# A hybrid layer with 32 experts on one core: the rows of the first four experts picked by one-hot products instead of gathered

## What is computed

```python
h = h + (merged @ w_out) * valid[None, :, None]
xn2 = rms_norm(h, norm2_w).reshape(B * T, D)
y_ffn = hier_moe(xn2, router_group, router_expert, expert_w_gate, expert_w_up, expert_w_down)
return h + y_ffn.reshape(B, T, D) * valid[None, :, None]

def hier_moe(xn, router_group, router_expert, w_gate, w_up, w_down):
    g_logits = xf @ router_group
    g_idx = jnp.argmax(g_logits, axis=-1)
    e_logits = ...                          # the 8 experts of the chosen group
    top_v, top_i = lax.top_k(e_logits, 2)
    for g in range(4):
        hg = silu(einsum('nd,edf->nef', xn, w_gate[g])) * einsum('nd,edf->nef', xn, w_up[g])
        y = y + einsum('nef,efd->nd', hg * combine[:, g, :, None], w_down[g])
```

## Time and profile before

| | |
|---|---|
| median of 3 runs | 680.68 us (679.83 to 681.95) |
| profiled execution | 684.17 us, its span 682.4 us |
| mean granted TensorE clock | 0.979 |
| busy share: PE, PEld, DVE, ACT, POOL | 95%, 73%, 56%, 30%, 15% |
| HBM read and written | 139.67 MB, 4.19 MB |
| chain that ended last, by engine | PE 86%, DVE 7%, ACT 3%, DMA 2%, issue 2% |

### The profile page before, as it was taken

One profiled execution on the slowest core, in us unless ns is written; L12 is line 12 of the kernel. 1 busy time (PEld: TensorE's weight loads), 2 busy tenths in 40 slices (PEclk: granted clock), 3 DMA queues, 4 the chain that ended last, 5 costly groups with the idle time before them and its releaser, 6 DMA issues.

```text
span 682.4 us, 11048 instructions
## 1 busy us (share of the span) xinstructions
PE 650.3 (95%) x4419; PEld 499.7 (73%) x4419; DVE 383.4 (56%) x729; ACT 202.2 (30%) x426; POOL 104.4 (15%) x142
## 2 busy tenths in 40 slices
PE   4999999999999999999999976999999999999997
PEld 2579999998888888888789963665757575656564
DVE  3648334678897878776764463452525344351514
ACT  5337132224534344432433350212020202010111
POOL 3300006899300000000000011110101001010010
PEclk9699999999999999999999995999999999999999
DMA  7431212301231111211553028999999999999953
GB/s 238 144 123 52 74 62 76 112 1 62 85 101 62 62 63 62 62 62 62 175 205 145 33 70 341 396 414 405 409 407 407 411 396 422 402 418 388 420 214 123
DMA packets 50086, 139.32 MB, mean 204 GB/s; under 512 B 6355, under 2 KB 28388, under 8 KB 41845
## 3 DMA queue, kind: packets, MB, share of 16 engines
q1 hardware_dynamic: 47298, 134.37, 51.6%
q0 software_dynamic: 2592, 4.20, 1.7%
q10 hardware_dynamic: 146, 0.07, 0.1%
HBM read 139.67 MB, written 4.19 MB: 211 GB/s over the span
## 4 chain that ended last, share of the span: by engine, by line
PE 86%; DVE 7%; ACT 3%; DMA 2%; issue 2%; POOL 0%; ACTq 0%; DVEq 0%; POOLq 0%
PE bank L917 17%; PE bank L583 12%; PE bank L584 12%; PE bank L585 12%; PE bank L930 8%; PE bank L1035 8%; PE bank L799 1%; DVE y_lo L1770 1%; PE bank L591 1%; PE bank L826 1%; PE bank L823 1%; PE bank L592 1%; ACT whi L1142 1%; DMA xg<-rows_hbm,row_no 1%; DVE sig_a L1504 1%
## 5 line engine op out<-in xcount | busy, mean ns | idle before, releaser
L1435 DVE TENSOR_TENSOR wlo<-wraw,whi 128x2048 fp32r<-128x2048 f32 (+1 forms) x25 | 56.5, 2258 | 19.8 <-ACT whi L1142 19.8
L583 PE MATMUL bank<-xhi,whi 128*128 128x512 f32 x160 | 64.5, 403 | 0.0
L583 PE MATMUL bank<-whi,xhi 128*128 128x256 f32 x224 | 64.4, 288 | 0.0
L584 PE MATMUL bank<-xlo,whi 128*128 128x512 f32 x160 | 63.3, 396 | 0.0
L584 PE MATMUL bank<-wlo,xhi 128*128 128x256 f32 x224 | 63.0, 281 | 0.0
L585 PE MATMUL bank<-whi,xlo 128*128 128x256 f32 x224 | 62.9, 281 | 0.0
L585 PE MATMUL bank<-xhi,wlo 128*128 128x512 f32 x160 | 62.9, 393 | 0.0
L917 PE MATMUL bank<-wgate,xgT 128*64 128x256 f32 x512 | 61.0, 393 | 1.3 <-DVE xgT L1728 1.0
L917 PE MATMUL bank<-wup,xgT 128*64 128x256 f32 x512 | 58.4, 381 | 0.0
L930 PE MATMUL bank<-wdown,hT 128*64 128x512 f32 x256 | 58.1, 595 | 0.0
L917 PEld LDWEIGHTS bank<-wgate,xgT 128*64 128x64 f32 x512 | 37.6, 142 | 22.5 <-issue 6.6
(11 more groups left out here) (313 smaller groups left out, 1321.0 us busy)
## 6 DMA issues: line engine op xcount, KB each, us to landing
wgate<-in_expert_w_gate SPq DMA_DIRECT2D x32, 1024.0 KB
wup<-in_expert_w_up SPq DMA_DIRECT2D x32, 1024.0 KB
wdown<-in_expert_w_down SPq DMA_DIRECT2D x32, 1024.0 KB, 17.8
wraw<-in_w_in SPq DMA_DIRECT2D x17, 1024.0 KB, 5.3
wraw<-in_w_out SPq DMA_DIRECT2D x4, 1024.0 KB, 5.0
h<-in_x SPq DMA_DIRECT2D x4, 512.0 KB, 5.8
wraw<-in_w_gla_branch SPq DMA_DIRECT2D x2, 1024.0 KB, 5.1
wraw<-in_w_attn_branch SPq DMA_DIRECT2D x2, 1024.0 KB, 5.2
```

The source lines that it names most:

```text
L583: nc.tensor.matmul(ps, lhi(k), rhi(k), start=(k == 0), stop=False)
L584: nc.tensor.matmul(ps, lhi(k), rlo(k), start=False, stop=False)
L1435: nc.vector.tensor_tensor(wl, raw, wh.bitcast(F32), ALU.subtract).then_inc(s_lo, 1)
```

## The change

The rows of the first body's four experts are no longer gathered from memory but picked on the chip. Three kinds of steps join the list. rowhi (ScalarE) writes a block of scaled rows, rounded to fp32r, into mhi, feature chunk by feature chunk (by_chunk reads h with a stride of 8 elements); rowlo (VectorE) writes the rest into mlo. pick (VectorE) turns a block's counts into ranks and builds its one-hot of 256 slots, onehot_r, in fp32r. select (TensorE) multiplies each of the eight feature chunks of mhi and then of mlo by the block's one-hot, sixteen products of 128x256 a block, summed over the four blocks in banks 1, 2, 3 and 5. The result is already transposed; VectorE and ScalarE weigh halves of it straight into xgT. Ranks are made block by block (all earlier blocks by ones, the own one by the triangle), and the totals that count the rounds in a product group of their own in bank 0. ScalarE casts the one-hots to bf16 for the transposes and slot products.

The gathers of body 0, its row numbers and its row transposes go; the storing of block 3's rows comes later on ScalarE (scaled_rows(3), behind the one-hots' move out); the slot weights of body 0 stand after the first gate product. At the end of a round eight further row transposes a pair with their moves by VectorE and ScalarE prepare the next round, whether or not there is one. The gate and up loads of pair 1 wait only for chunk 1 of block 3 (unit 13), the three down loads for the picks and casts; in the sync queue they stand behind the store of block 3's rows (store_rows(b) is the wait of L1082 and the store of L1083). In SBUF xgT and ident_b change places, and onehot_r lies in the buffer of pair 0's second down weight.

```diff
+        s += [("pick", (n - 9) // 4)] if n >= 9 and n % 4 == 1 else []
+        s += [("rowhi", (n - 6) // 4)] if n >= 6 and n % 4 == 2 else []
+        s += [("rowlo", (n - 7) // 4)] if n >= 7 and n % 4 == 3 else []
         s += [("route", (n - 5) // 4)] if n >= 5 and n % 4 == 1 else []
         s += [("weigh", (n - 6) // 4)] if n >= 6 and n % 4 == 2 else []
-    s += [("hT", 15), ("rstd", 3), ("logit", 14), ("logit", 15), ("rank", 2), ("route", 3), ("rank", 3)]
+    s += [("rank", 2), ("hT", 15), ("pick", 2), ("rstd", 3), ("logit", 14), ("logit", 15)]
+    s += [("select", b) for b in range(3)] + [("route", 3), ("rowhi", 3), ("rank", 3), ("pick", 3), ("rowlo", 3), ("select", 3)]
...
                 elif kind == "rank":
                     b = step[1]
-                    pe.wait_ge(s_choice, b + 1)
-                    if b == 0:
+                    if b:
+                        pe.wait_ge(s_ohr, b)
+                    else:
                         pe.wait_ge(s_tri, 1)
                         rank_ps = banks.take(pe, "O", "rank")
-                    nc.tensor.matmul(rank_ps[:, b * NE:(b + 1) * NE], tri_r[:, :], chosen[:, b, :], start=(b == 0), stop=False)
-                    later = NB - b
-                    last = nc.tensor.matmul(rank_ps[:, (b + 1) * NE:(NB + 1) * NE].rearrange("p (a e) -> p a e", e=NE), ones[:, :],
-                                            chosen[:, b:b + 1, :].to_broadcast([P, later, NE]), start=False, stop=(b == NB - 1))
+                    for a in range(b):
+                        nc.tensor.matmul(rank_ps[:, b * NE:(b + 1) * NE], ones[:, :], chosen[:, a, :], start=(a == 0), stop=False)
+                    pe.wait_ge(s_choice, b + 1)
+                    nc.tensor.matmul(rank_ps[:, b * NE:(b + 1) * NE], tri_r[:, :], chosen[:, b, :],
+                                     start=(b == 0), stop=True).then_inc(s_ranked, 1)
                     if b == NB - 1:
-                        last.then_inc(s_ranked, 1)
+                        pe.wait_ge(banks.free[TOTAL_BANK], banks.uses[TOTAL_BANK])
+                        for a in range(NB):
+                            last = nc.tensor.matmul(tiles[TOTAL_BANK][:, 0:NE], ones[:, :], chosen[:, a, :],
+                                                    start=(a == 0), stop=(a == NB - 1))
+                        last.then_inc(s_total, 1)
+                elif kind == "select":
+                    b = step[1]
+                    if b == 0:
+                        for k in PICK_BANKS:
+                            pe.wait_ge(banks.free[k], banks.uses[k])
+                    for part, t in enumerate((mhi, mlo)):
+                        pe.wait_ge(s_rowlo if part else s_rowhi, b + 1)
+                        pe.wait_ge(s_ohr, b + 1)
+                        for g in range(4):
+                            for j in range(2):
+                                last = nc.tensor.matmul(tiles[PICK_BANKS[g]][:, j * 2 * P:(j + 1) * 2 * P],
+                                                        t[:, 2 * g + j, b * P:(b + 1) * P], onehot_r[:, b, :],
+                                                        start=(b == 0 and part == 0 and j == 0), stop=(b == NB - 1 and part == 1 and j == 1))
+                            if b == NB - 1 and part == 1:
+                                last.then_inc(s_pick[g], 1)
...
-                pe.wait_ge(s_info, NB + 1)
-                for k in range(4):
-                    pe.wait_ge(s_add[k], r * (2 * BODIES) + 1)
-                for s in range(2):
-                    pe.wait_ge(s_idx[s], r * BODIES + 1)
-                    last = slot_matmul(s, 0, 2, 8)
-                last.then_inc(s_pwm, 1)
-                row_transposes(0, (0,))
...
                         last_scatter(i, n)
+                        row_transposes(i + 1)
...
-            sp.wait_ge(*banks.emptied(("unit", NCHUNK - 1, NB - 1)))
-            load(1, 1, True, (0,))
-            for s in range(2):
-                sp.wait_ge(s_xg[s], 16)
-            load(1, 1, True, (1,))
+            for b in range(NB - 1):
+                store_rows(b)
+            sp.wait_ge(*banks.emptied(("unit", WO + 1, NB - 1)))
+            load(1, 1, True)
+            store_rows(NB - 1)
+            sp.wait_ge(s_pick[3], 1)
+            sp.wait_ge(s_cast, 2)
             load(0, 0, False, (1,))
             load(1, 1, False)
...
+                elif kind == "rowhi":
+                    b = step[1]
+                    if b == NB - 1:
+                        act.wait_ge(s_ohr, b)
+                        nc.scalar.activation(onehot[:, 0:b, :], onehot_r[:, 0:b, :].bitcast(F32), ACT.Copy).then_inc(s_cast, 1)
                     act.wait_ge(s_r2, b + 1)
-                    nc.scalar.activation(xs[b % 2][:, :].rearrange("p (k c) -> p c k", k=KT),
-                                         h[:, b, :].rearrange("p (c k) -> p c k", k=KT), ACT.Copy,
-                                         scale=b1[:, b, 5:6]).then_inc(s_xs_loc[b], 1)
+                    nc.scalar.activation(mhi[:, :, b * P:(b + 1) * P], by_chunk(b), ACT.Copy,
+                                         scale=b1[:, b, 5:6]).then_inc(s_rowhi, 1)
...
+            act.wait_ge(s_ohr, NB)
+            nc.scalar.activation(onehot[:, NB - 1, :], onehot_r[:, NB - 1, :].bitcast(F32), ACT.Copy).then_inc(s_cast, 1)
+            for s in range(2):
+                for k in range(4, KT):
+                    act.wait_ge(s_pick[k // 2], 1)
+                    last = nc.scalar.activation(xgT[:, k, s * P:(s + 1) * P],
+                                                tiles[PICK_BANKS[k // 2]][:, (k % 2) * 2 * P + s * P:(k % 2) * 2 * P + (s + 1) * P],
+                                                ACT.Copy, scale=norm2[:, k:k + 1])
+                last.then_inc(s_xgT[2 * s + 1], 1)
...
-            onehot_out(0, 0)
+            act.wait_ge(s_ohTm[1], 1)
+            onehot_out(0, 0, first_flipped)
+            scaled_rows(NB - 1)
...
+                elif kind == "pick":
+                    b = step[1]
+                    dve.wait_ge(s_ranked, b + 1)
+                    ps = banks.get("rank")
+                    moved = nc.vector.scalar_tensor_tensor(rank[:, b, :], ps[:, b * NE:(b + 1) * NE], 1.0,
+                                                           chosen[:, b, :].bitcast(F32), ALU.add, ALU.mult)
+                    if b < NB - 1:
+                        link(moved)
+                    else:
+                        moved.then_inc(s_rank, 1)
+                        dve.wait_ge(s_rank, 2)
+                    full = [P, 4, SLOT]
+                    nc.vector.tensor_tensor(onehot_r[:, b, :].rearrange("p (e t) -> p e t", e=4),
+                                            C("slots").unsqueeze(1).to_broadcast(full), bc(rank[:, b, 0:4], full),
+                                            ALU.is_equal).then_inc(s_ohr, 1)
+                elif kind == "rowlo":
+                    b = step[1]
+                    dve.wait_ge(s_rowhi, b + 1)
+                    cb = slice(b * P, (b + 1) * P)
+                    nc.vector.scalar_tensor_tensor(mlo[:, :, cb], by_chunk(b), b1[:, b, 5:6], mhi[:, :, cb].bitcast(F32),
+                                                   ALU.mult, ALU.subtract).then_inc(s_rowlo, 1)
...
+            for s in range(2):
+                for g in range(2):
+                    dve.wait_ge(s_pick[g], 1)
+                    picked = tiles[PICK_BANKS[g]][:, :].rearrange("p (k t) -> p k t", k=2)[:, :, s * P:(s + 1) * P]
+                    last = nc.vector.tensor_tensor(xgT[:, 2 * g:2 * g + 2, s * P:(s + 1) * P], picked,
+                                                   bc(norm2[:, 2 * g:2 * g + 2], [P, 2, P]), ALU.mult)
+                last.then_inc(s_xgT[2 * s], 1)
...
-                gather(0, s, 0)
```

96 lines of the change are left out of this document (63 added, 33 removed).

## The result

| | before | after |
|---|---|---|
| median of 8 runs each on the same chip | 681.56 us (679.83 to 684.60) | 678.40 us (676.21 to 679.25) |
| profiled execution, its span | 684.17 us, 682.4 us | 676.36 us, 674.5 us |
| mean granted TensorE clock | 0.979 | 0.997 |
| busy share: PE, DVE, ACT, POOL | 95%, 56%, 30%, 15% | 97%, 58%, 32%, 15% |

After over before is 0.9948, 95% interval 0.9929 to 0.9966: 3.2 us faster by the medians, where 6.5 were forecast. The forecast of 674.2 us missed by 4.2, and its range ended at 678.0. The changed kernel's eight executions lie in two groups: three at 676.2 to 676.4 us with a mean clock of 0.997, and five at 678.3 to 679.3 with 0.995. The profiled one is of the first group.

The account below looks back on a forecast made before the run. The handover from output projection to experts was taken as the bound. Gains of 3.1 + 2.6 + 0.8 = 6.5 us took the profiled 684.17 to 677.7, less the 3.5 profile-to-median difference: 674.2 us, range 672.2 to 678.0.

Parts of the forecast that it names:

- the sum's first term: Handover up to the first gate product: it starts at 416.1 against 419.21, 3.1 us gained.
- the way from the profiled execution to the median: Before's profiled execution stood 3.5 above its median of 680.68; that difference was carried over, turning 677.7 into 674.2 us.
- Part 1: Ahead of the last unit: block 2's scaling, 2.1 us, delays the exponentials; last add ends at 404.1 instead of 401.97.
- Part 2: Picks of blocks 0 to 2: 5.8 us, TensorE done at 411.5, the work of VectorE and ScalarE hidden beside them.
- 48 picks 0.12 us apart: Sign that the forecast is right: picks of blocks 0 to 2 start at this spacing from 405.7.
- the clock falls in the gap: Rival, chance 0.11: clock falls in TensorE's gap 401.3 to 405.7, low for 5.9 us, costing 3.0; gain 3.5, 677.2.
- Part 3: Block 3's ranks, picks, moves and loop entry: mlo at 1.28 us, first gate product at 416.1, 3.1 us gained.
- Part 4: Clock and body 0: clock stays at 2.4 GHz, 2.6 us gained on first gate product; transposes gone, 0.8 gained.
- Parts 5 and 6: Transfers: down loads issued near 421.3, no wait on weights. Tail: about 2.2 us added beside the output transfer, costing nothing, at most 1.0.

Follow-up runs that it names:

- the head filled: Unused transposes (41) in TensorE's waits of the first 22 us, added to the changed kernel: 676.93 us; the same added to before: 680.05 us.
- the run with further products: Unused products in TensorE's handover waits: 14 and 4 added to the changed kernel, 675.34 us; 75 added to before, 679.15 us.
- a run that could have told half a microsecond: Best version (both orders, 41 head transposes, 671.38 us) without the end-of-round preparation, sixteen row transposes and ten moves: 671.66 us.

## Why the forecast was too good

The gathers' latency went as forecast; the size was off. The step that failed is the sum's first term, "3.1 us gained" up to the first gate product: it came out as 0.86. Two prices in it were wrong, the clock during the picks (put at full, it fell: 1.1 us) and the strided low part mlo (1.28 put, 2.15 measured: 0.87); 0.2 are smaller links. A second step, the way from the profiled execution to the median, failed too. The first column is the forecast less the 3.43 us by which the head was shorter:

| | forecast | measured |
|---|---|---|
| exponentials of block 2 | 397.4 | 397.36 |
| last residual add ends | 400.7 | 400.49 |
| first pick | 402.3 | 402.26 |
| 48th pick done | 408.1 | 409.21 |
| block 3's last pick done | 411.6 | 413.57 |
| first gate product | 412.7 | 414.92 |
| second pair's gate product | 421.0 | 423.17 |

**Part 1 was right.** The scaling took 2.27 us where I put 2.1, and it headed the chain as forecast. But I counted the gap that it opens on TensorE for its length alone, 1.85 us; the clock that fell behind it cost at least 1.40 more.

**Part 2 failed in its clock.** "48 picks 0.12 us apart" was 0.23 for the first eight and 0.17 for the next: 1.1 us late. This is the rival "the clock falls in the gap", to which I gave 0.11 because dense products follow at once. They do not prevent the fall; they pay for it until the clock is back. Nor is the fall fixed: behind the same wait it lasted 3.4 us in both profiles of the changed kernel and with the head filled (where a second of 3.4 followed at the last picks), 6.8 in the run with earlier rank products, and there was none in the one with the low part first. The Trainium skill, "TensorE: Matmul & The Clock Gate", section "The HAM clock gate (the "warmup" mystery)", holds that the engine drops after idling and recovers only after sustained work. The traces agree, with the size left to them: 1.40 us here by the run with further products and 1.74 by the one with the low part first, against the 3.0 that the rival had.

**Part 3 failed in the price of mlo.** I took 1.28 us for the strided read, from the contiguous row, and it was 2.15 (0.87 dearer, the wait of 0.81). By the run without the stride, 0.87 is also what the way from block 3's rank products to the gate product loses by it (5.71 us, 4.84 without). The Trainium skill, "SBUF — State Buffer", section "Door 1: The DMA port swizzle", says that accesses crossing to a new 16-byte line pay a penalty. I weighed this and set it aside; it was right here: by the run without the stride both engines pay for it, VectorE by a factor of 1.67 and ScalarE by 1.96. That VectorE's rows are slower per element to begin with, my reason for the cheap value, did not shield it. The last 0.2 us are the way from the last pick to the gate product, 1.35 instead of 1.1, with its wait for ScalarE's moves.

**Part 4 came out, in the part that it named.** The gate product took 3.67 us, and from it to the second pair's 8.25 instead of 11.74: 3.49 gained, 3.4 forecast. What all of the clock cost before's handover is 3.29 by the run with further products, a little more than my 2.6. But I booked it as a gain in full, and the changed kernel gives 1.40 back in the logits and the first picks. Without any fall in them the handovers are 26.61 and 24.15: of the 4.35 us, 2.46 are work and latency that went, and 1.89 are clock. That split is for this pair of profiles; two further profiles of before with nothing added in the handover have 28.85 and 29.60 us there, not 29.90, so the clock's share differs by up to 1 us between executions.

**Parts 5 and 6 were right.** The down loads were issued at 420.65, 2.8 us later than forecast (421.3 less 3.4), 2.2 of it the handover's own delay, and still TensorE waited for no weights: 251.3 us from the second pair on, as before. The tail cost nothing, by a run that could have told half a microsecond.

**From profile to median** a further step failed. I carried 3.5 us over from before's profiled execution as if it were an offset of profiling. It was not: 0.9 of it is the median of three runs, which eight runs put at 681.56, and that execution lost 2.6 us to a low clock in its head, where a typical one loses about 1.5. Its handover was 0.3 to 1.05 us longer than in the two other profiles just named; what is left, 0.5 to 1.2 us, no run explains. The changed kernel's profiled execution lost nothing in the head and stands 2.0 under its median. So the handover's miss of 2.1 us makes half of the 4.2. The other half is before's median, 0.9 higher in eight runs than in three, and about 1.2 by which the typical execution gains less than the pair of profiles: 3.1 us between the kernels with a filled head, 3.2 without. This last term is no larger than the scatter, since the repeat of the changed kernel has 4.5 in its place. The slower executions of the changed kernel would be those with a second or longer fall; their mean clock of 0.995 is also that of the two profiles that show one. By size it would lie in the head, where a fall cost 1.6 to 3.1 us, since the second fall at the last picks lengthened the handover by 0.5 only (26.09 against 25.55), and the slower group stands 2 to 3 us above the other. Against it, five of six executions with a filled head still have 0.995. No profile of the group itself was taken, so its cause stays open.

**Where the rest of the idea was.** The waits of 3.3 us for the rows and 3.0 for the choice did go, but the scaling ahead of the last unit's add, the slow picks and the low part took most of it back ahead of the gate product. A list order in which ScalarE's exponentials come first gives 3.4 us more on the handover, rank products of block 3 between picks 1.1 more.

## What to carry to other kernels

Where a change puts new work on a side engine, look for the operation on the critical chain that now queues behind it, and try the other order before judging the change: here that order was worth as much as the change itself. A gap of TensorE must be priced twice, for its own length and for the slow products behind it, and cheap work placed in it shows at once which of the two is being paid. Before forecasting a median from one profiled execution, find out what that execution lost to a low clock, since that is a draw and not an offset.

## What the runs showed of the hardware

- The granted clock fell behind single waits of TensorE of 1.85 and, in the one profile that has it, 0.71 us in the handover, and behind two of 0.39 and 0.79 us some 1.2 us apart. Behind the first and the last of these it fell in some executions and not in others.
- The profile's granted clock missed a fall in one profile: it read 1.00 for a stretch in which 128x512 products came 0.43 us apart instead of 0.23. The spacing of like products is the safer row.
- A read of fp32 with a stride of 32 bytes cost ScalarE 2246 ns against 1143 for 128x1024, and VectorE 2130 against 1275.
- One-hot picks of 128x256 in fp32r with a new weight tile each ran 0.113 to 0.118 us apart at the full clock: 40 in a row at 0.113 in the run with exponentials first, 32 at 0.118 in the changed kernel.
